# Five moves of work in a pooling and retention step: states, k and v, gates, pooling sums, stores

## The chip, the cores and the metric

The kernel runs on 1 core of one Trainium2 chip. The metric is the device time in microseconds, the median of several runs. Lower is better.

## What is computed

One step of a hybrid decoder layer, for a prompt of 2048 tokens and for 8 sample sequences of 4 new tokens each, all in float32:

```python
h = rmsnorm(x, g_norm)
u_p, z_p, q, k, v, z_r, gates = split(h @ w_in)        # widths 1024,1024,1024,1024,2048,2048,2048
pooled = windowed means of u_p (windows 2, 4, 8, 16; one per group of 256) - u_p
pooled = einsum(pooled, w_pool_group) * pool_scale
y_pool = (pooled * silu(z_p)) @ w_branch_pool
o, s_new = retention(rope(q), rope(k) * 256**-0.5, v, s_old)   # 4 heads, Dk 256, Dv 512
y_ret = (groupnorm(o) * gn_ret * silu(z_r)) @ w_branch_ret
merged = sigmoid(gate_p) * y_pool + sigmoid(gate_r) * y_ret
y = rmsnorm(x + merged @ w_out, g_final)               # also returned: the last 15 rows of u, s_new
```

The prompt begins with empty states. The samples begin with `state_pool` (8 x 15 x 1024) and `state_ret` (8 x 4 x 256 x 512, 16 MB), and the new states are stored.

## The kernel before

**How it works.** Every product is made of float32r matmuls on split operands: high part, and low part = value - high. One product of 128 x 128 weights by 512 tokens takes three matmuls. ScalarE makes the high parts, VectorE the low ones. All engines run programs written out by hand in a fixed order, and semaphores that count finished steps tie them together. There are three stages.

**Stage A** (to about 1656 us of the span) projects the prompt through `w_in`. It runs over two halves of 1024 tokens and, in each, 40 jobs of 256 columns: per head q, v, k, v, zp, u, z, z, and eight gate jobs. A job is seven block products (a Strassen-like scheme; slots 0 to 6 are A11B11, A12B21, S2T2, S1T1, S3T3, S4B22, A22T4) of twelve matmuls each. VectorE's program at each slot i is: evict the product of this slot (slots 1, 4, 5), make the low part of the weights six products ahead, then a piece of the post-processing of the job before. ScalarE does likewise (evictions at 0, 2, 3, 6; highs of weights; sigmoids). The last product (slot 6) writes the bank that slot 4's eviction empties (`c22_done`); slot 2 (S2T2) waits for ScalarE's copy of slot 0's product (`part_s`, `s_copied`). For a "u" job, VectorE computes windowed sums in `windows(j, t, first, end)`: steps k = 0 to g (head g) are sums over shifted copies, k = g + 1 is the final that writes `c_out`; step 0 also copies 16 columns. The second part of tokens (t = 1) is handled during the next job, a z job. That z job's `z_sigmoid(j, 0)`, at the end of slot 6 on ScalarE, writes `tmp`, which shares its place with `win_a` and `win_b`, so it waits for the final. Results go to DRAM (`qk_d`, `kt_d`, `v_d`, `z_d`, `pool_d`, `zp_d`, `gate_d`).

**Stage B** (to about 2752 us) runs over four blocks of 512 tokens. Per head: `update(hb, 0)`, `output(hb, 0)`, `turn_og(hb - 1)` (transposes), `update(hb, 1)`, `branch(hb - 1, 0)`, `output(hb, 1)`, `scores(hb + 1)`, `branch(hb - 1, 1)`; hb counts heads over all blocks. Behind the last head come group mixing, the branch and the output projections. `gate_og(hb)` on VectorE multiplies four banks of transposed outputs by the gate z (line 2261) and makes their low parts; the high parts are ScalarE's. `branch(hb, 0)` overwrites those four banks, so it waits for all four gatings, and before quarter vt for its low part. SyncE issues the loads in program order; a wait holds all that is behind it. At the passage from A to B it loads head 1's q and k^T scores operands, four weight units, stores the last gate, waits for everything, and only then loads head 1's k and v for the updates (`head_piece(0, 1, 2..5)`).

**The samples' stage** (from about 2752 us) runs over four heads. Per head: panels of weights come through a ring of eight buffers `s_w` (SyncE); TensorE multiplies them by the tokens; the states `s_in` (8 samples, 512 KB each) are read by the output matmuls (line 1573), updated by VectorE with TensorE's `update`, multiplied by a decay on ScalarE (`scaled(h, q)`, into one of four buffers `s_out`), and stored by GpSimd, which waits for each scaling. Before sample 0 to 3 of the next head ScalarE waits (`s_stored`) until GpSimd has seen all stores land; before sample 4 to 7 until the store of four samples before has. Behind `scaled(h, 4)` ScalarE makes the highs of the z panel. The tail projects and normalises the samples.

Of the kernel before, what the change touches and what calls it, by code (L numbers as in the profile page):

```python
# [208 lines left out]
def build(nc, io):  # L209
    with ExitStack() as ctx:  # L210
# [302 lines left out]
        s_stored = Steps(sem("s_stored"), [], in_heads(["states"]), [])  # L513
# [162 lines left out]
        def _(sp):  # L676
# [226 lines left out]
            for what in ("q", "k"):  # L903
                stored(sp, max(j for j in range(ALL) if JOBS[j] == (what, 1, 0)))
            for n in range(2):
                head_piece(0, 1, n)
            for n in range(RAW):
                unit(0, n)
            store(ALL - 1)
# [11 lines left out]
            head_gates(0, 0)  # L921
# [3 lines left out]
            for n in range(2, 6):  # L925
                head_piece(0, 1, n)
# [3 lines left out]
            for n in range(RAW, LEAD):  # L930
                unit(0, n)
# [103 lines left out]
            results(NB - 1)  # L1035
# [3 lines left out]
            load_states(0, seqs)  # L1039
            for h in range(HEADS):  # L1040
                if h:
                    load_qkv(h)
                    load_states(h, (7,))
                if h == HEADS - 1:
                    for k in range(4):
                        load_pair(pair("mix", None, k), io["w_pool_group"][0, k], GW)
                load_columns("z", h, h * DV + COL_ZR)
                for p in range(2):
                    name, first = (("u", COL_U), ("zp", COL_ZP), ("gp", COL_G), ("gr", COL_G + D))[h]
                    load_columns(f"{name}{p}", None, first + 512 * p)  # L1050
                    load_states(h + 1, ((0, 1, 2), (3, 4))[p])
                for p in range(2):
                    for k in range(2):
                        load_pair(pair("br", h, 2 * p + k),
                                  io["w_branch_ret"][0][h * DV + k * 2 * P:h * DV + (k + 1) * 2 * P, p * 512:(p + 1) * 512])
                load_states(h + 1, (5, 6))
                if h == 0:
                    sp.wait_ge(out_stored, 16 * NT * NB)
                    sp.dma_start(s_gate_b[:].rearrange("p g c -> p (g c)"), io["b_gate"].broadcast_to([S, 2 * D]))\
                        .then_inc(s_gate_in, 16)  # L1060
                    sp.dma_start(s_pool_s[:], io["pool_scale"].broadcast_to([S, D])).then_inc(s_gate_in, 16)
# [6 lines left out]
        def _(pool):  # L1068
# [92 lines left out]
            for s in (s_pow, s_stored):  # L1161
                pool.sem_inc(s.sem, s.credit)
# [17 lines left out]
            for h in range(HEADS):  # L1180
# [3 lines left out]
                for q in seqs:  # L1184
                    if q == 5:
                        inverse_std("head", h, "var_eps")
                    pool.wait_ge(s_act.sem, s_act.done("head", h, f"scaled{q}"))
                    pool.dma_start(io["ret_sample"][0, q, h].rearrange("(k p) v -> p k v", p=P), s_out[:, q % 4])\
                        .then_inc(s_state_out[q % 4], 16)

                if h + 1 < HEADS:
                    pool.dma_start(s_c[:], io["c_sample"][h + 1]).then_inc(s_c_in, 16)
                    pool.dma_start(s_decay[:], io["c_sample_decay"][h + 1]).then_inc(s_c_in, 16)
                for k in range(4):
                    pool.wait_ge(s_state_out[k], (h + 1) * (16 * SB // 4))
                pool.sem_inc(s_stored.sem, 1)
# [9 lines left out]
            pool.wait_ge(s_c_in, 32 * HEADS)  # L1206
            pool.wait_ge(out_stored, 16 * NT * NB)
# [406 lines left out]
        def _(act):  # L1614
# [321 lines left out]
            def scaled(h, q):  # L1936
                wait("head", h, f"new{q}_1")
                if q < 4:
                    act.wait_ge(s_stored.sem, s_stored.done("head", h, None))
                else:  # L1940
                    act.wait_ge(s_state_out[q % 4], h * (16 * SB // 4) + 16)
                do(s_out[:, q % 4], s_in[:, q], scale=s_decay[:, 0:1])

# [43 lines left out]
        def _(dve):  # L1987
# [173 lines left out]
            for j in range(ALL):  # L2161
                for i in range(PROD):
# [4 lines left out]
                    if j and kind(j - 1) == "u":  # L2167
                        if i < 3:
                            windows(j - 1, 0, 2 + i, 3 + i)
                        elif i == 3:  # L2170
                            windows(j - 1, 1, 0, 2)
                        else:
                            windows(j - 1, 1, i - 2, i - 1)
# [81 lines left out]
            def gate_og(hb):  # L2255
                s, h = hb % 2, hb % HEADS
                dve.wait_ge(z_arrived[s], 32 * (hb // 2 + 1))
                for vt in range(5):
                    if vt < 4:
                        dve.wait_ge(ogt_mm, 4 * hb + vt + 1)  # L2260
                        dve.scalar_tensor_tensor(out=z_in[s][:, vt, :], in0=banks[2 + vt][:],  # L2261
                                                 scalar=ret_g[:, h, vt:vt + 1], in1=z_in[s][:, vt, :],
                                                 op0=ALU.mult, op1=ALU.mult).then_inc(og_gated, 1)
                    if vt:
                        dve.wait_ge(og_hi_done, 4 * hb + vt)
                        tt(z_lo[s][:, vt - 1, :], z_in[s][:, vt - 1, :], og_hi[:, vt - 1, :].bitcast(F32),
                           ALU.subtract, og_lo_done)
# [334 lines left out]
            for p, bank in enumerate((4, 5)):  # L2602
# [5 lines left out]
                if p == 0:  # L2608
                    lows_of("out0", None, range(3))
# [40 lines left out]
```

## Time and profile before

| | |
|---|---|
| median of 3 runs | 3061.72 us (3061.45, 3061.72, 3066.86) |
| the profiled execution | 3067.94 us, span 3066.2 us |
| TensorE matmul busy | 2969.4 us, 97% |
| VectorE busy | 1875.3 us, 61% |
| ScalarE busy | 1183.9 us, 39% |
| GpSimd busy | 710.7 us, 23% |
| HBM | read 410.63 MB, written 169.50 MB, 189 GB/s over the span |
| chain that ended last | TensorE 83%, VectorE 7%, DMA 5%, issue 3% |

A row of the timeline gives the start, the length, the engine, the line of the kernel, the operation with its output and inputs, and in brackets the idle time of the engine before it and who ended it. SPq and POOL DMA rows are issues, not transfers. Matmuls are pipelined: rows overlap, and the time that one takes from the engine is the distance of two starts.

### The profile page before, as it was taken

How to read it: one execution, taken by the hardware profiler on the slowest of the kernel's cores; microseconds unless marked ns; L12 is line 12 of the kernel's file. 1: busy time of each engine (PE TensorE's matmuls, PEld its weight loads, DVE VectorE, ACT ScalarE, POOL GpSimd, SP SyncE). 2: the span in 40 equal slices, each digit the busy share in tenths (PEclk: the TensorE clock that was granted, in tenths of full speed). 3: DMA queues.
4: the chain of work that ended last, by engine and by line, in shares of the span. 5: the costliest groups of instructions: out<-in, count | busy, mean ns of one | idle time of the engine just before them, and what ended most of it. 6: DMA issues, size and time to landing. Idle time of an engine off the chain costs nothing.

```text
span 3066.2 us, 35792 instructions
## 1 busy us (share of the span) xinstructions
PE 2969.4 (97%) x13064; PEld 2303.6 (75%) x13064; DVE 1875.3 (61%) x2625; ACT 1183.9 (39%) x1925; POOL 710.7 (23%) x501
## 2 busy tenths in 40 slices
PE   6999999999999999999999999999999999998997
PEld 5888888888778888888887888888888888872332
DVE  8666576765464756566665674657567566653435
ACT  5434444445554444443443333323333333332223
POOL 5242524344332344343432000000000000001110
PEclk9999999999999999999999999999999999999999
DMA  4535354436543453444446546635554564649885
GB/s 133 206 121 189 131 186 145 165 128 201 186 165 124 151 179 138 163 156 156 160 163 238 221 160 246 275 133 186 228 221 151 219 253 163 212 158 367 304 307 210
DMA packets 297542, 582.14 MB, mean 190 GB/s; under 512 B 24777, under 2 KB 167625, under 8 KB 286192
## 3 DMA queue, kind: packets, MB, share of 16 engines
q1 hardware_dynamic: 292039, 562.73, 51.8%
q0 software_dynamic: 5328, 17.12, 1.4%
q8 instruction: 106, 1.74, 0.2%
q14 instruction: 69, 0.56, 0.1%
HBM read 410.63 MB, written 169.50 MB: 189 GB/s over the span
## 4 chain that ended last, share of the span: by engine, by line
PE 83%; DVE 7%; DMA 5%; issue 3%; ACT 1%; POOL 1%; SPq 0%; DVEq 0%; ACTq 0%; POOLq 0%
PE bank L1224 25%; PE bank L1226 24%; PE bank L1225 24%; PE bank L1512 4%; DMA raw<-in_w_branch_pool 2%; PE bank L1573 2%; PE bank L1272 1%; DMA s_w<-in_w_in 1%; DVE z_in L2261 1%; DVE win_a L1989 1%; DVE wa_lo L1989 1%; DVE z_lo L1989 1%; DVE c_out L1989 1%; PE bank L1566 1%; DVE xs L2003 1%
## 5 line engine op out<-in xcount | busy, mean ns | idle before, releaser
L1224 PE MATMUL bank<-xa_hi,wa_hi 128*128 128x512 f32 x2240 | 885.4, 395 | 12.5 <-DVE c_out L1989 8.1
L1226 PE MATMUL bank<-xa_hi,wa_lo 128*128 128x512 f32 x2240 | 875.4, 391 | 0.0
L1225 PE MATMUL bank<-xa_lo,wa_hi 128*128 128x512 f32 x2240 | 874.7, 390 | 0.0
L1224 PEld LDWEIGHTS bank<-xa_hi,wa_hi 128*128 128x128 f32 x2240 | 421.8, 188 | 100.5 <-issue 15.8
L1226 PEld LDWEIGHTS bank<-xa_hi,wa_lo 128*128 128x128 f32 x2240 | 421.4, 188 | 88.8
L1225 PEld LDWEIGHTS bank<-xa_lo,wa_hi 128*128 128x128 f32 x2240 | 421.9, 188 | 83.7
L1989 DVE TENSOR_TENSOR wa_lo<-w_raw,wa_hi 128x512 fp32r<-128x512 f32 x320 | 313.0, 980 | 192.9 <-ACT wa_hi L1667 191.4
L1989 DVE TENSOR_TENSOR wa_lo<-w_sum,wa_hi 128x512 fp32r<-128x512 f32 x240 | 195.2, 813 | 224.6 <-ACT wa_hi L1667 224.6
L1989 DVE TENSOR_TENSOR w_lo<-raw,w_hi 128x512 fp32r<-128x512 f32 (+1 forms) x288 | 180.4, 660 | 221.4 <-ACT w_hi L1775 221.2
L1667 ACT ACTIVATE wa_hi<-w_raw 128x512 fp32r<-128x512 f32 x320 | 200.9, 628 | 245.7 <-PE bank L1226 242.1
L1775 ACT ACTIVATE w_hi<-raw 128x512 fp32r<-128x512 f32 (+1 forms) x288 | 165.7, 603 | 270.8 <-PE bank L1226 102.7
L1156 POOL TENSOR_TENSOR inv_std<-var_eps,half 128x2 f32<-128x2 f32 x32 | 25.7, 802 | 943.2 <-DVE var_eps L2246 943.2
L1108 POOL TENSOR_TENSOR w_sum<-w_raw,w_sum 128x512 f32<-128x512 f32 x80 | 127.1, 1588 | 382.3 <-DVE wa_lo L1989 380.4
L1224 PE MATMUL bank<-og_hi,w_hi 128*128 128x512 f32 x512 | 205.0, 400 | 9.2 <-DVE z_in L2261 9.2
L1225 PE MATMUL bank<-z_lo,w_hi 128*128 128x512 f32 x512 | 203.0, 396 | 0.0
L1226 PE MATMUL bank<-og_hi,w_lo 128*128 128x512 f32 x512 | 201.8, 394 | 0.0
L1667 ACT ACTIVATE wa_hi<-w_sum 128x512 fp32r<-128x512 f32 x240 | 150.4, 627 | 122.3 <-PE bank L1226 115.2
L1114 POOL TENSOR_TENSOR w_sum<-w_raw,w_sum 128x512 f32<-128x512 f32 x80 | 105.7, 1322 | 289.6 <-DVE wa_lo L1989 289.6
L1120 POOL TENSOR_TENSOR c_out<-c_out,tmp 128x1024 f32<-128x1024 f32 x48 | 118.7, 2475 | 196.1 <-ACT tmp L1711 196.1
L1989 DVE TENSOR_TENSOR c_out<-bank,part_s 128x512 f32<-128x512 f32 x144 | 99.0, 687 | 96.5 <-PE bank L1226 64.9
L1103 POOL TENSOR_TENSOR w_sum<-w_raw 128x512 f32<-128x512 f32 x80 | 124.2, 1553 | 73.1 <-DVE wa_lo L1989 64.9
L1110 POOL TENSOR_TENSOR w_raw<-w_raw 128x512 f32<-128x512 f32 x80 | 134.0, 1674 | 0.0
(261 smaller groups left out, 4711.7 us busy)
## 6 DMA issues: line engine op xcount, KB each, us to landing
w_raw<-in_w_in SPq DMA_DIRECT2D x80, 1024.0 KB, 5.1
v_d<-turned SPq DMA_DIRECT2D x64, 512.0 KB, 3.2
qk_s<-qk_d SPq DMA_DIRECT2D x32, 1024.0 KB, 7.5
v_s<-v_d SPq DMA_DIRECT2D x32, 1024.0 KB, 10.9
raw<-in_w_branch_ret SPq DMA_DIRECT2D x128, 256.0 KB, 3.9
s_w<-in_w_in SPq DMA_DIRECT2D x64, 512.0 KB, 8.6
tabs<-in_c_rope SPq DMA_DIRECT2D x16, 1024.0 KB, 6.6
qk_d<-high SPq DMA_DIRECT2D x32, 512.0 KB, 4.6
```

Of the source, the lines that this page charges most:

```text
L1103: pool.tensor_tensor(w_sum[:, 0], b12, b11, ALU.subtract).then_inc(w_summed, 1)
L1108: pool.tensor_tensor(w_sum[:, 1], b22, w_sum[:, 0], ALU.subtract).then_inc(w_summed, 1)
L1110: pool.tensor_tensor(b12, b22, b12, ALU.subtract).then_inc(w_summed, 1)
L1114: pool.tensor_tensor(w_sum[:, 1], b21, w_sum[:, 1], ALU.subtract).then_inc(w_summed, 1)
L1120: pool.tensor_tensor(c_out[:, j % 2, t], c_out[:, j % 2, t], tmp[t][:], ALU.mult).then_inc(z_mul, 1)
L1224: pe.matmul(out, lh, rh, start=first, stop=False, skip_group_check=onto)
L1225: pe.matmul(out, lh, rl, start=False, stop=False, skip_group_check=onto)
L1226: return pe.matmul(out, ll, rh, start=False, stop=last, skip_group_check=onto)
L1512: mm = pe.matmul(banks[bank][0:lhs.shape[-1], at_col:at_col + width], lhs, s_w[:, m % SRING, k % 2, 0:width], start=first, stop=last)
L1667: act.activation(wa_hi[:, n % SLOTS], src, ACT.Copy).then_inc(wa_hi_done, 1)
L1775: act.activation(w_hi[:, u % RING, 0:width], raw[:, u % RAW, 0:width], ACT.Copy).then_inc(w_hi_done, 1)
L1989: return dve.tensor_tensor(out, a, b_, op).then_inc(s, 1)
```

## The change

Five edits, on the same computation.

- **Stage A, pooling sums** (t = 1): at slot 3 only step 0 (before: 0 and 1), at slots 4 and 5 steps 1 and 2 (before: 2 and 3), at slot 6 steps 3 and 4 (before: 4).
- **A to B, SyncE's order**: head 1's q, k, and k, v of its first chunk, then head 0's gate, the last store, four weight units, k and v of the second chunk; the waits for everything come behind these. The wait for the stores of head 1's q and k jobs goes.
- **Stage B, `gate_og`**: four gatings, then four low parts, in place of gate, gate, low, gate, low, gate, low, low.
- **Samples, SyncE**: `load_states(0, ...)` comes before the stores of the last block's results. **Samples, ScalarE**: each scaling is followed by a wait for its own end and the issue of its store, on ScalarE's queue; GpSimd no longer issues these 32 stores, and the semaphore `s_stored` is gone: ScalarE waits only for the store that used the same buffer.
- **Tail, VectorE**: the third low part of the out0 weights comes behind the second half of `s_g` in place of behind the first.

```diff
-            for what in ("q", "k"):
-                stored(sp, max(j for j in range(ALL) if JOBS[j] == (what, 1, 0)))
-            for n in range(2):
+            for n in range(4):
                 head_piece(0, 1, n)
+            head_gates(0, 0)
+            store(ALL - 1)
             for n in range(RAW):
                 unit(0, n)
-            store(ALL - 1)
+            for n in range(4, 6):
+                head_piece(0, 1, n)
...
             sp.wait_ge(win_step, win_steps(NS, 0, 0))
-            head_gates(0, 0)
             stored(sp, ALL - 2)
             stored(sp, ALL - 1)
             all_turned_stored(sp, ALL)
-            for n in range(2, 6):
-                head_piece(0, 1, n)
+            for n in range(RAW, LEAD):
+                unit(0, n)
...
-            results(NB - 1)
             sp.wait_ge(m_added, KT * NB)
             sp.wait_ge(pg_lo_done, KT * NB)
             sp.wait_ge(mix_mm, KT * NB)
             load_states(0, seqs)
+            results(NB - 1)
...
-                for q in seqs:
-                    if q == 5:
-                        inverse_std("head", h, "var_eps")
-                    pool.wait_ge(s_act.sem, s_act.done("head", h, f"scaled{q}"))
-                    pool.dma_start(io["ret_sample"][0, q, h].rearrange("(k p) v -> p k v", p=P), s_out[:, q % 4])\
-                        .then_inc(s_state_out[q % 4], 16)
-
+                inverse_std("head", h, "var_eps")
+
+                pool.wait_ge(s_act.sem, s_act.done("head", h, f"scaled{SB - 1}"))
...
-                for k in range(4):
-                    pool.wait_ge(s_state_out[k], (h + 1) * (16 * SB // 4))
-                pool.sem_inc(s_stored.sem, 1)
...
                 wait("head", h, f"new{q}_1")
-                if q < 4:
-                    act.wait_ge(s_stored.sem, s_stored.done("head", h, None))
-                else:
-                    act.wait_ge(s_state_out[q % 4], h * (16 * SB // 4) + 16)
+                if h or q >= 4:
+                    act.wait_ge(s_state_out[q % 4], 16 * (2 * h + q // 4))
                 do(s_out[:, q % 4], s_in[:, q], scale=s_decay[:, 0:1])
+                wait("head", h, f"scaled{q}", s_act)
+                act.dma_start(io["ret_sample"][0, q, h].rearrange("(k p) v -> p k v", p=P), s_out[:, q % 4])\
+                    .then_inc(s_state_out[q % 4], 16)
...
                         if i < 3:
                             windows(j - 1, 0, 2 + i, 3 + i)
-                        elif i == 3:
-                            windows(j - 1, 1, 0, 2)
                         else:
-                            windows(j - 1, 1, i - 2, i - 1)
+                            windows(j - 1, 1, i - 3, i - 2 if i < PROD - 1 else GROUPS + 1)
...
-                for vt in range(5):
-                    if vt < 4:
-                        dve.wait_ge(ogt_mm, 4 * hb + vt + 1)
-                        dve.scalar_tensor_tensor(... z_in[s][:, vt, :] ...).then_inc(og_gated, 1)
-                    if vt:
-                        dve.wait_ge(og_hi_done, 4 * hb + vt)
-                        tt(z_lo[s][:, vt - 1, :], ..., ALU.subtract, og_lo_done)
+                for vt in range(4):
+                    dve.wait_ge(ogt_mm, 4 * hb + vt + 1)
+                    dve.scalar_tensor_tensor(... z_in[s][:, vt, :] ...).then_inc(og_gated, 1)
+                for vt in range(4):
+                    dve.wait_ge(og_hi_done, 4 * hb + vt + 1)
+                    tt(z_lo[s][:, vt, :], ..., ALU.subtract, og_lo_done)
...
                 if p == 0:
-                    lows_of("out0", None, range(3))
+                    lows_of("out0", None, range(2))
+            lows_of("out0", None, (2,))
             wait("tail", 0, "m_t", s_act)
```

## Rows read from the trace of the kernel before

**Rows 1.** View by line, TensorE: busy us, mean ns, idle before and releasers.
```profile
L1224 PE MATMUL bank<-xa_hi,wa_hi 128*128 128x512 f32 x2240 | 885.4, 395 | 12.5 <-DVE c_out L1989 8.1 <-ACT part_s L1674 3.4 <-DVE wa_lo L1989 0.8
...
L1224 PE MATMUL bank<-og_hi,w_hi 128*128 128x512 f32 x512 | 205.0, 400 | 9.2 <-DVE z_in L2261 9.2
```

**Rows 2.** Timeline 1611 to 1623 (start us, length us), behind a pooling job.
```profile
1612.23 1.25 DVE L1989 TENSOR_TENSOR win_b<-win_a 128x1050 f32<-128x1050 f32 x1
...
1612.66 0.39 PE L1225 MATMUL bank<-xa_lo,wa_hi 128*128 128x512 f32 x1
...
1612.88 0.39 PE L1226 MATMUL bank<-xa_hi,wa_lo 128*128 128x512 f32 x1
...
1613.40 0.68 DVE L1989 TENSOR_TENSOR c_out<-bank,part_s 128x512 f32<-128x512 f32 x1
...
1614.22 0.47 PE L1224 MATMUL bank<-xa_hi,wa_hi 128*128 128x512 f32 x1 [0.95 <-DVE c_out L1989]
...
1618.41 0.69 DVE L1989 TENSOR_TENSOR wa_lo<-w_raw,wa_hi 128x512 fp32r<-128x512 f32 x1 [0.24 <-ACT wa_hi L1667]
...
1619.11 1.22 DVE L2121 SCALAR_TENSOR_TENSOR c_out<-win_b,ext 128x1024 f32<-128x1024 f32 x1
...
1621.68 0.58 ACT L1674 ACTIVATE part_s<-bank 128x512 f32<-128x512 f32 x1
```

**Rows 3.** Timeline, gating of two prompt heads, at 1958 and 2083.
```profile
1958.18 1.41 DVE L2261 SCALAR_TENSOR_TENSOR z_in<-bank,ret_g,z_in 128x512 f32<-128x512 f32 x2
...
1959.63 0.69 DVE L1989 TENSOR_TENSOR z_lo<-z_in,og_hi 128x512 fp32r<-128x512 f32 x1
...
1961.23 0.39 PE L1226 MATMUL bank<-v_s,kt_s 128*128 128x512 f32 x1
...
1962.30 0.50 PE L1224 MATMUL bank<-og_hi,w_hi 128*128 128x512 f32 x1 [0.68 <-DVE z_in L2261]
...
2083.67 0.49 PE L1224 MATMUL bank<-og_hi,w_hi 128*128 128x512 f32 x1 [0.19 <-DVE z_in L2261]
```

**Rows 4.** Timeline 1673 to 1694, heads 0 and 1 of block 0.
```profile
1673.33 1.43 SPq L862 DMA_DIRECT2D v_s<-v_d  x1
...
1675.74 0.69 DVE L1989 TENSOR_TENSOR sc<-bank,mask 128x512 f32<-128x512 f32 x1 [0.74 <-PE bank L1226]
...
1680.65 0.79 PE L1224 MATMUL bank<-v_s,kt_s 128*128 128x512 f32 x1 [4.94 <-DMA v_s<-v_d]
...
1684.86 0.69 DVE L2221 COPY state<-bank 128x512 f32<-128x512 f32 x1
...
1689.63 1.41 DVE L2261 SCALAR_TENSOR_TENSOR z_in<-bank,ret_g,z_in 128x512 f32<-128x512 f32 x2
...
1693.75 0.50 PE L1224 MATMUL bank<-og_hi,w_hi 128*128 128x512 f32 x1 [0.69 <-DVE z_in L2261]
```

**Rows 5.** Stretches (last: PEclk, DMA share, GB/s), then timeline lines.
```profile
2754.00:2756.00 2.00, 2.00 (x6) 0.85 (x5) 2.00 (x2) 0.00 (x0) 2.00 (x4) 1.00 0.05 14
...
2759.18 5.91 SPq L1029 DMA_DIRECT2D s_in<-in_state_ret  x8
...
2824.16 6.23 PE L1512 MATMUL bank<-s_w,sx 128*128 128x512 f32 x7 [5.77 <-DMA s_w<-in_w_in]
```

**Rows 6.** Timeline 2774 to 2787, samples' head 0; then DMA landings (us).
```profile
2774.33 1.15 ACT L1843 ACTIVATE s_out<-s_in,s_decay 128x1024 f32<-128x1024 f32 x1 [6.16 <-DVE s_in L2343]
...
2785.38 3.89 ACT L1930 ACTIVATE s_hi<-s_w 128x1024 fp32r<-128x1024 f32 x4
...
2786.71 4.62 DVE L1989 TENSOR_TENSOR s_lo<-s_w,s_hi 128x1024 fp32r<-128x1024 f32 x4
...
out_ret_sample<-s_out POOLq DMA_DIRECT2D x8, 512.0 KB, 6.8
...
DMA to landing us min/median/max: 3.9/10.6/17.2
```

**Rows 7.** Timeline 3040, the samples' tail.
```profile
3040.33 0.68 PE L1448 MATMUL bank<-ident,s_g 32*128 32x32 f32 x8 [3.31 <-DVE s_g L2343]
```

More of the change, by code:

```diff
@@ L512, in build @@
         s_pow = Steps(sem("s_pow"), ["x"], in_heads(["o"]), ["out"])
-        s_stored = Steps(sem("s_stored"), [], in_heads(["states"]), [])
         s_mm = Steps(sem("s_mm"), ["x_t", "hist"],
@@ L929, in _ @@
                 .then_inc(b_consts_in, 16)
-            for n in range(RAW, LEAD):
-                unit(0, n)
             def ahead(b, first, end):
@@ L1158, in _ @@
                             inverse_out(b - 1)
-            for s in (s_pow, s_stored):
-                pool.sem_inc(s.sem, s.credit)
+            pool.sem_inc(s_pow.sem, s_pow.credit)
             def inverse_std(part, h, name):
@@ L1206, in _ @@
             pool.wait_ge(s_c_in, 32 * HEADS)
+            for k in range(4):
+                pool.wait_ge(s_state_out[k], HEADS * (16 * SB // 4))
             pool.wait_ge(out_stored, 16 * NT * NB)
@@ L2257, in gate_og @@
                 dve.wait_ge(z_arrived[s], 32 * (hb // 2 + 1))
-                for vt in range(5):
-                    if vt < 4:
-                        dve.wait_ge(ogt_mm, 4 * hb + vt + 1)
-                        dve.scalar_tensor_tensor(out=z_in[s][:, vt, :], in0=banks[2 + vt][:],
-                                                 scalar=ret_g[:, h, vt:vt + 1], in1=z_in[s][:, vt, :],
-                                                 op0=ALU.mult, op1=ALU.mult).then_inc(og_gated, 1)
-                    if vt:
-                        dve.wait_ge(og_hi_done, 4 * hb + vt)
-                        tt(z_lo[s][:, vt - 1, :], z_in[s][:, vt - 1, :], og_hi[:, vt - 1, :].bitcast(F32),
-                           ALU.subtract, og_lo_done)
+                for vt in range(4):
+                    dve.wait_ge(ogt_mm, 4 * hb + vt + 1)
+                    dve.scalar_tensor_tensor(out=z_in[s][:, vt, :], in0=banks[2 + vt][:],
+                                             scalar=ret_g[:, h, vt:vt + 1], in1=z_in[s][:, vt, :],
+                                             op0=ALU.mult, op1=ALU.mult).then_inc(og_gated, 1)
+                for vt in range(4):
+                    dve.wait_ge(og_hi_done, 4 * hb + vt + 1)
+                    tt(z_lo[s][:, vt, :], z_in[s][:, vt, :], og_hi[:, vt, :].bitcast(F32), ALU.subtract, og_lo_done)
             def add_y(hb, p):
```

## The prediction

> **What bounds the kernel now.** I read the share of busy time first, then TensorE's groups by line with the idle time before them, then the list of TensorE's gaps in its timeline, and around each kind of gap the timeline of all engines; for the samples' stage also the DMA share by stretch. TensorE is busy 97% of the span, so only its gaps can be won or lost. The two largest kinds that a releaser explains by VectorE stand in [rows 1]: 8.1 us behind the evictions of line 1989 in stage A and 9.2 us behind the gating of line 2261. The rest that matters here are single waits for DMA (4.94 us in [rows 4], 5.77 us in [rows 5]) and one of 3.31 us in the tail [rows 7]. In the prompt stages matmuls start 0.22 to 0.23 us apart [rows 2], so a gap costs its start-to-start time less 0.23.
>
> **Pooling sums.** There are 8 "u" jobs (4 heads, 2 halves), and in the job behind each TensorE stops once. [rows 2] show the last: the sum k=1 (1612.23, 1.25 us) sits ahead of the eviction of product S3T3 (1613.40, 0.68), whose bank the last product wants at 1612.88 + 0.23 = 1613.11; it starts at 1614.22. Loss 1.11 us. The change moves k=1 behind that eviction, which can then start at 1612.2 and end at 1612.8: no wait. What is late next is the end of the sums. For heads 0 and 1 they end before the last product and cost nothing. For head 2 the final moves into the last product (slot 6): a low of weights waits for ScalarE, which follows TensorE; it starts 4.19 us after the last product's start (1618.41 against 1614.22), the final starts 0.70 later (1619.11), lasts 1.22, and ScalarE's copy to part_s starts 1.35 after its end (1621.68) and lasts 0.58. That is 8.04 us after the last product's start, plus about 0.15 for the semaphore; the product that needs it starts after 3 x 12 x 0.2275 = 8.19. Just hidden. For head 3 one more sum (1.2 us) is in slot 6: 9.2 to 9.4, so TensorE waits about 1.0 there. It waits at the next job's third product for ScalarE, which stands in front of z_sigmoid for tmp. So 6 jobs win 1.11 and 2 win 0.1 to 0.2: **7.0 us** (ends: 4.8 if head 2 is late too, 8.9 if none is).
>
> **Gates in one piece.** [rows 3]: gating starts at 1958.18 and today runs gate, gate, low, gate, low, gate, with 0.66 us between starts of gates and 0.61 behind a low; TensorE starts 4.12 us later (1962.30), once all four banks are read. Now it is four gates (2.64) and one low (0.61 to 0.69, +0.05): 3.35 to 3.4, so 1961.55. It could have started at 1961.23 + 0.23 = 1961.46. Win 0.75. The later lows come every 0.61 us, TensorE takes 2.7 us for each, and VectorE's whole chain of eight operations keeps its length, so who is queued behind (bias, state_low) sees no change. There are 12 such gaps of 1.07 to 1.11 us (three heads, four blocks): 9.0. The four last heads have a smaller one (2083.67, idle 0.19; start to start 0.58): the whole gap of 0.35 goes, 1.4. Sum **10.4 us** (8 to 11).
>
> **Head 1's k and v.** SyncE issues v at 1673.33, behind a wait for the last gate's store; TensorE is ready at 1675.55 and starts at 1680.65 [rows 4]. After the change k and v are issued at about 1656.6, behind 3.5 MB of other loads; at the 400 GB/s of a full stretch they are in by 1671. That wait of 5 us goes, but what is late next is VectorE: it masks head 1's scores until 1675.74 + 0.69, which TensorE waits for too (start 1676.5), then has the statistics of head 0 and four lows of branch weights, and copies the new state at 1684.86 without having waited for TensorE. The two copies, two bn_stats and their small operations need 0.6 + 0.6 + 0.6 + 1.03 = 2.85 us, so gating starts at 1687.7 instead of 1689.63. Win **1.9 us**, not 5; with the one-piece gates branch(0, 0) starts at 1691.1, not 1693.75. z_in and the four weight units, moved among these loads, land by about 1678, and are wanted from 1681.8 on: nothing. Ends 1 and 5.
>
> **Samples' states sooner.** The DMA engines are idle at 2754 to 2756 (share 0.05), between the load of q, k, v and the results' stores; the states follow at 2759.18 [rows 5]. From 2758 to 2824 they are full, and TensorE's waits for s_w (1.1 us in the u panels, 1.5 at the branch, 5.9 before head 1's q and k at 2824.16) come at the end of that backlog. Issued at 2747.4, the states fill the hole: shares of 0.88, 0.05, 0.74 over three stretches of 2 us leave 2.7 us of DMA time, and all that stands behind comes 2.7 us sooner. The stores of results move behind the states and nobody waits for them. What is left of the last wait (5.9 less what does not reach it) still takes the clock down (granted 0.50, that is 1.2 GHz, in 2824 to 2828). Win **2.7 us** (0 to 7: with the clock kept, 4 more).
>
> **Stores from ScalarE.** The trace has no DMA issued by ScalarE. SyncE's issue of the same shape takes 5.91/8 = 0.74 in a burst [rows 5], 0.37 at least. Per sample ScalarE then needs 1.15 + 0.1 + 0.37 to 0.74, below the 2.5 us in which TensorE delivers samples. But behind scaled(4) stand the highs of z: hi at 2785.38, low at 2786.71, TensorE at 2788.27, almost without slack [rows 6]. One wait for its own end and one issue put 0.5 to 0.8 us ahead of them; 0.3 of it was slack of VectorE in heads 0 to 2, none in head 3. Cost 3 x 0.25 + 0.55 = **1.3 us** (0 to 5, the upper end with issues of 1.3 us). The three scalings of samples 5 to 7 grow by 2 us, with 7 us before their reader. GpSimd's queue only loses work; s_c and s_decay keep their place in time.
>
> The row says that landing depends on the queue: 6.8 us median on GpSimd's, 10.6 for states on SyncE's. The Trainium skill, "DMA: Bandwidth & Descriptors", section "Issuing engines are not separate DMA queues", says that DMAs of all engines share the same 16 DMA engines and that issuing from another engine saves only issue time. By it this part wins nothing in bandwidth, which is also what the sum has; by a reading in which the stores went faster the sum would be lower by what DMA waits are left, up to 5 us.
>
> **Tail.** One low of 4.62/4 = 1.15 us [rows 6] leaves the place ahead of s_g of half 1, for which TensorE waits 3.31 us [rows 7]; it now runs while TensorE transposes and ScalarE copies s_mt (0.7 + 0.4 us). Win **1.1 us** (0.9 to 2.6; the matmuls behind it run 0.63 instead of 0.39 long, at half the clock, and a shorter wait may spare that).
>
> **Sum.** 7.0 + 10.4 + 1.9 + 2.7 - 1.3 + 1.1 = 21.8 us. All gains of the prompt stages lie in local chains that start at TensorE, so each passes on to the end. The profiled execution took 3067.94 us (span 3066.2) and would take 3046; it is 6.2 above the median of the runs, 3061.72, which the forecast goes by: **3040 us**.
>
> **Rivals.** (1) ScalarE's issues are dear, or head 2's pooling is late too: 3.7 + 2.2 us less won, 3046, with runs to 3050. For it: no row of such an issue, slack of 0.0 to 0.1. (2) More than the sum: the clock is kept at 2824 and in the tail, 4 + 1.5 us more, 3034. Against it: of the wait at 2824 more than 3 us stay. (3) Slower: ScalarE's stores land as late as SyncE's loads when queued, up to 17.2 us [rows 6]. scaled(4) needs the buffer of sample 0; its store is issued about 2775.6 and today's start is 2784.33, so it hides landings up to 8.7 us. At 17.2 each head loses 8.5, four heads 34: 3074. It decides from (L - 8.7) x 4 = 22, L = 14.2. Against it: ScalarE never has more than two or three stores queued, and heads 1 to 3 begin with DMA engines half idle. (4) The moves don't do what they say: pooling stops only change their place for all heads, and the DMA hole is filled by nothing useful: 7 + 2.7 less, 3050 to 3056.
>
> **Chances.** Forecast 0.60 (3035 to 3045), (1) 0.18, (2) 0.10, (3) 0.03, (4) 0.09. Range 3031 to 3053: it takes in (1), most of (2) and half of (4), and the 5 us by which the runs shown differ only in part. 0.2% is 6.1 us, about what a measurement of this kernel can tell from no change; faster by more than that (under 3055.6) 0.92, within 0.05, slower 0.03.
>
> **What would show it.** In the changed trace: the gap at the last product behind u jobs gone, and a gap of about 1 us before the third product of the next job for head 3 only, released by part_s; gaps at branch(hb, 0) of 0.3 us, released by a low; update(1, 0) starting at the mask's end and branch(0, 0) 2.6 us earlier; the DMA share without a hole, the wait before head 1's q and k still 5 to 6 us; z highs 0.6 us later in each sample head; the tail's wait near 2.2 us. The prediction is wrong if ScalarE's s_out waits for DMA, or if gaps of 1 us come back at another product of stage A.

## The result and the profile after

The changed kernel takes 3040.76 us (median of four runs, 3038.15 to 3046.85), before 3061.72: a ratio of 0.9925, interval 0.9911 to 0.9939, so 0.6 to 0.9% faster. On a second chip the unchanged file gave 3041.37 against 3065.37 (0.9919, 0.9905 to 0.9933). The profiled execution took 3038.15 us, span 3036.4, against 3067.94 and 3066.2. As before's profiled run lay above its median and this one below, 29.8 us separate the two traces, and only 21 to 24 the medians. A second profile of the changed kernel (the run e12_after_again) has a span of 3040.2; where one stretch is read closely, both are given.

The view by line has lost the two kinds of gaps of [rows 1]. Columns: count, busy us, mean ns of one, idle us before them and releasers. The matmuls of line 1224 are at line 1215 now:

```profile
PE 2962.3 (98%) x13064; PEld 2300.4 (76%) x13064; DVE 1873.1 (62%) x2625; ACT 1185.8 (39%) x1925; POOL 688.6 (23%) x469
...
L1215 PE MATMUL bank<-xa_hi,wa_hi 128*128 128x512 f32 x2240 | 884.3, 395 | 6.3 <-ACT part_s L1665 5.2 <-DVE wa_lo L1981 1.0
...
L1215 PE MATMUL bank<-og_hi,w_hi 128*128 128x512 f32 x512 | 204.2, 399 | 1.0 <-DVE y L2262 0.7 <-issue 0.2
```

c_out and z_in have gone as releasers (8.1 and 9.2 us). part_s went from 3.4 to 5.2, which is the new wait behind the pooling jobs of head 3.

TensorE's marks, the same instruction found in each trace (us; the last column is the sum of the prediction split in the same way):

| stretch | before | after | after again | won | forecast |
|---|---|---|---|---|---|
| start to head 0's first v_s, kt_s matmul (stage A) | 1659.26 | 1651.61 | 1653.69 | 7.7, 5.6 | 7.0 |
| to branch(0, 0) | 34.49 | 31.85 | 31.82 | 2.6, 2.7 | 2.6 |
| to the samples' first panel | 1058.65 | 1049.76 | 1049.86 | 8.9, 8.8 | 9.7 |
| to head 1's q and k panel | 71.76 | 68.49 | 68.17 | 3.3, 3.6 | 2.7 |
| to the tail's s_g transposes | 216.17 | 212.87 | 213.26 | 3.3, 2.9 | -0.2 |
| to the last matmul | 14.00 | 12.51 | 14.09 | 1.5, -0.1 | 0 |
| to the issue of y_sample's store | 4.71 | 4.76 | 4.76 | 0 | 0 |
| to the end of the span | 7.12 | 4.51 | 4.50 | 2.6, 2.6 | 0 |

Two stretches won what the sum did not have: the one to the tail and the end of the span. The rows of after that answer to those of before, all of the timeline (start us, length us, in brackets idle before and releaser). First head 3's pooling, at the third product of the next job [rows 2], then the crossing to stage B [rows 4]:

```profile
667.87 0.47 PE L1215 MATMUL bank<-xa_hi,wa_hi 128*128 128x512 f32 x1 [0.71 <-ACT part_s L1665]
...
1614.87 0.47 PE L1215 MATMUL bank<-xa_hi,wa_hi 128*128 128x512 f32 x1 [1.00 <-ACT part_s L1665]
...
1693.69 1.28 ACT L1766 ACTIVATE w_hi<-raw 128x512 fp32r<-128x512 f32 x2 [6.46 <-DMA raw<-in_w_branch_ret]
1698.91 1.16 ACT L1766 ACTIVATE w_hi<-raw 128x512 fp32r<-128x512 f32 x2 [3.93 <-DMA raw<-in_w_branch_ret]
...
1703.32 0.50 PE L1215 MATMUL bank<-og_hi,w_hi 128*128 128x512 f32 x1 [0.69 <-DVE y L2262]
```

The rows show the wait of about 1 us that was forecast, and one that wasn't: the branch weights land late behind head 1's k and v, ScalarE's highs come in two late pairs, VectorE's y behind them, and TensorE stops at 1703.32 (0.97 us from start to start, so 0.74 is handed back; 0.76 idle in the second profile).

Then the samples' stage: head 1's q and k panel [rows 5] with the clock around it (last columns of a stretch: granted clock, DMA share, GB/s), head 3's z panels, and the tail [rows 7]:

```profile
2801.71 2.93 PE L1503 MATMUL bank<-s_w,sx 128*128 128x512 f32 x3 [5.10 <-DMA s_w<-in_w_in]
...
2798.00:2802.00 4.00, 0.29 (x1) 0.29 (x2) 0.00 (x0) 0.00 (x0) 0.40 (x1) 0.64 1.10 317
2802.00:2806.00 4.00, 4.00 (x5) 1.55 (x5) 0.00 (x0) 0.00 (x0) 0.00 (x0) 0.50 1.10 337
...
2734.00:2736.00 2.00, 2.00 (x6) 0.88 (x5) 1.35 (x2) 0.00 (x0) 2.00 (x4) 1.00 0.95 377
...
2973.65 0.39 PE L1521 MATMUL bank<-s_hi,sx_hi 128*32 128x512 f32 x1 [1.10 <-DVE s_lo L1981]
...
3014.58 0.62 PE L1439 MATMUL bank<-ident,s_g 32*128 32x32 f32 x7 [1.80 <-DVE s_g L2331]
```

The DMA hole is filled (0.95 in the stretch that answers to the 0.05 of before). The wait of 5.8 us is now 5.1 (4.8 in the second profile) and the granted clock still falls to 0.50 behind it. ScalarE's stores, of which before had no row (the group of all 32, issue ns min/median/max, then the landing us):

```profile
L1933 ACTq DMA_DIRECT2D out_ret_sample<-s_out x32: 378/379/467, 2756.3 to 2984.3; - x32
...
DMA to landing us min/median/max: 2.8/7.5/10.9
...
  ACT s_out L1834: 4.1, 8
  ACT s_hi L1921: 2.0, 4
```

An issue costs 0.38 to 0.47 us. The last two lines say who waited for a scaling: ScalarE itself, 0.5 us before each of the eight scalings that nothing else delayed, and 0.5 before each of the four s_hi. In this kernel no scaling waits for a DMA.

### The profile page after: what moved, and what is told of

It is laid out like the page before. It is cut to its first block, busy times and chain, and to the rows that moved or that the text cites. A ratio compares the mean times of both kernels' runs of the same rounds, so it can differ in the third digit from the quotient of the medians.

```text
span 3036.4 us, 35782 instructions
## 1 busy us (share of the span) xinstructions
PE 2962.3 (98%) x13064; PEld 2300.4 (76%) x13064; DVE 1873.1 (62%) x2625; ACT 1185.8 (39%) x1925; POOL 688.6 (23%) x469
## 4 chain that ended last, share of the span: by engine, by line
PE 87%; DMA 4%; DVE 4%; issue 2%; ACT 1%; POOL 1%; SPq 1%; ACTq 0%; DVEq 0%; POOLq 0%
PE bank L1215 26%; PE bank L1217 26%; PE bank L1216 25%; PE bank L1503 4%; DMA raw<-in_w_branch_pool 2%; PE bank L1564 2%; PE bank L1263 1%; DMA s_w<-in_w_in 1%; PE bank L1371 1%; DVE wa_lo L1981 1%; PE bank L1557 1%; DMA raw<-in_w_branch_ret 1%; DVE xs L1995 1%; DVE xa_lo L1981 0%; PE bank L1521 0%
```

## The experiments

The theory is that of the prediction: the parts are local, and their gains add up. The rivals are that parts take their gain from one another, or that the gain beyond the sum belongs to one of them. e1 to e4 ran on one chip, where before took 3063.91 us, e5 to e8 on another with 3066.01, e9 to e12 on a third with 3065.37, so times of different chips are compared by their ratio to before. A gain in us is one minus that ratio, times before's median.

**Pooling alone** (before with this edit):

```diff
-                        elif i == 3:
-                            windows(j - 1, 1, 0, 2)
                         else:
-                            windows(j - 1, 1, i - 2, i - 1)
+                            windows(j - 1, 1, i - 3, i - 2 if i < PROD - 1 else GROUPS + 1)
```

> The kernel before with the shift of the pooling sums alone. My theory (local waits, head 3's sums end too late): the six waits of about 1 us behind the u jobs of heads 0 to 2 go, the two of head 3 are replaced by waits for part_s of 0.7 and 1.0 us; stage A ends 7.0 to 7.7 us sooner, all of it reaches the end, 3054 to 3055 us. Rival (the stops only change their place): the waits come back for head 2 as well or for all heads, 0 to 5 us, 3057 to 3062.

Measured: 0.9975 (0.9965 to 0.9986), 7.7 us less (4.3 to 10.7). The line of stage A:

```profile
L1224 PE MATMUL bank<-xa_hi,wa_hi 128*128 128x512 f32 x2240 | 883.5, 394 | 6.6 <-ACT part_s L1674 5.9 <-DVE wa_lo L1989 0.6
```

8.1 us of c_out are gone, part_s is up by 2.5, and stage A ends at 1650.46 against 1659.26. The six profiles without this edit end stage A anywhere from 1659.3 to 1662.3 (mean 1660.4), and the six with it and no other edit of stage A from 1650.5 to 1655.1 (mean 1652.4). So one profile can't give the size to a microsecond; the means lie 8.0 us apart, one above the forecast of 7.0.

**Gates alone** (before with `gate_og` as four gatings and then four lows, as in the diff of the change):

> The kernel before with the gates in one piece alone. My theory: twelve waits of 0.7 us before branch(hb, 0) go but for some 0.1, and four of 0.2: 10 us, 3051 to 3052. In the first block head 1 hangs on VectorE's chain, which the order inside the gating does not shorten, yet its first low comes 0.75 earlier all the same. Rival (weights' loads or the later lows take the gain back, as the wait of 0.69 us before the second half of the branch in the changed kernel hints): up to 2 us less in each block, 3054 to 3058.

Measured: 0.9964 (0.9951 to 0.9977), 11.0 us less (7.0 to 15.0). z_in is gone as a releaser of branch matmuls:

```profile
L1224 PE MATMUL bank<-og_hi,w_hi 128*128 128x512 f32 x512 | 204.1, 399 | 0.1
```

Branch(0, 0) comes 0.76 us sooner after the start of stage B and the rest of the prompt takes 1049.32 in place of 1058.65: 10.1 us, for the 10.4 of the sum. The gaps of 0.3 us released by a low, which the prediction named as a sign, didn't come: 0.1 us is all the idle time of this line.

**Head 1's k and v alone** (before with the two parts of the diff that change SyncE's order at the crossing):

> The kernel before with SyncE's new order at the passage from stage A to B alone. My theory: the wait of 4.94 us for v goes, but VectorE's queue (mask, statistics, four lows, copies) sets the next start, so branch(0, 0) comes 1.9 us sooner and no more, 3059.8. Rival (the transfer was the bound): 5 us sooner at branch(0, 0), 3056.7. A third: what is gained is lost behind head 2's loads, which now meet the branch's weights sooner: 1 us or less.

Measured: 0.9994 (0.9985 to 1.0004), 1.8 us less with an interval on both sides of nothing; this and the next are below what the runs can settle, and the trace has to speak. TensorE's rows at the crossing:

```profile
1686.63 0.47 PE L1222 MATMUL bank<-v_s,kt_s 128*128 128x512 f32 x1 [2.37 <-DVE state L2219]
...
1692.14 0.50 PE L1222 MATMUL bank<-og_hi,w_hi 128*128 128x512 f32 x1 [0.93 <-DVE z_in L2259]
```

The DMA wait of 4.94 us is gone, a wait of 2.37 for VectorE's state stands in its place, and branch(0, 0) comes 1.98 us sooner after the start of stage B (32.51 against 34.49). In the kernels that keep the old order and the old gating this stretch runs from 33.0 to 34.6, as the wait for v_s varies (3.50 to 5.19).

That VectorE sets the new start, and not TensorE, can be read from the seven profiles with both this order and the new gating. In five of them the granted clock fell to 0.50 for some 2 us behind the wait of 2.37 us, in two (e10_store3_gpsimd and e11_store3_scalar) it stayed at 1.00 up to there, TensorE was ready sooner and waited for the gating:

```profile
1686.89 0.47 PE L1231 MATMUL bank<-og_hi,w_hi 128*128 128x512 f32 x1 [1.84 <-DVE z_in L2267]
```

Yet branch(0, 0) came 31.82 to 31.86 us after the start of stage B in all seven.

The wait for y at the branch's second half is 0.19 us here and is in no row of the run with the gates alone; only both together make it the 0.69 of the changed kernel. There two parts do take something from each other, about half a microsecond.

**States alone** (before with `load_states(0, ...)` ahead of the results):

```diff
-            results(NB - 1)
...
             load_states(0, seqs)
+            results(NB - 1)
```

> The kernel before with the samples' states ahead of the results' stores alone. My theory: 2.7 us of idle DMA time are filled, the waits for s_w before head 1's q and k end 2.7 to 3.3 us sooner, the last of them stays above 4 us and still takes the granted clock to 1.2 GHz for a while; 3058 to 3059. Rival (the hole is filled, but SyncE's queue or the DMA backlog gives it back): no change at head 1's q and k, 3061.7. Second rival (the clock is kept): 7 us, 3054.7.

Measured: 0.9996 (0.9987 to 1.0005), 1.2 us less. The hole is filled, and the panel waits less:

```profile
2754.00:2756.00 2.00, 2.00 (x6) 0.95 (x5) 1.92 (x2) 0.00 (x0) 2.00 (x4) 1.00 0.78 300
...
2820.61 1.22 PE L1512 MATMUL bank<-s_w,sx 128*128 128x512 f32 x1 [4.38 <-DMA s_w<-in_w_in]
```

From the first panel to head 1's q and k: 67.95 us. Over all profiles the kernels without this edit take 69.0 to 71.8 (mean of six 70.7), those with it in the changed kernel's order of loads 67.3 to 69.4 (mean of seven 68.4). So it is 2.3 us by the means, where the sum had 2.7, and single profiles of kernels alike in this stage differ by as much.

**Stores alone** (before with the stores on ScalarE's queue), and the reverse, **the changed kernel with the stores back on GpSimd**. In both GpSimd's program and `s_stored` change with it as in the change above; the lines on ScalarE are

```diff
                 do(s_out[:, q % 4], s_in[:, q], scale=s_decay[:, 0:1])
+                wait("head", h, f"scaled{q}", s_act)
+                act.dma_start(io["ret_sample"][0, q, h]..., s_out[:, q % 4]).then_inc(s_state_out[q % 4], 16)
```

> The kernel before with the 32 stores of new states issued by ScalarE alone. My theory: an issue costs ScalarE 0.4 to 0.5 us behind each scaling and 0.1 for its own end; heads 0 to 2 start z 0 to 0.3 us later, head 3 0.5 to 0.6; 1 us slower or the same, 3062 to 3063. Rival (the queue matters for the transfers: stores land sooner and weights too): the DMA waits before head 1 shrink, 3057 to 3060. Open from the two profiles: the end behind the last transfer took 4.4 us before and 1.8 after; if GpSimd's long list of DMAs is the cause, this kernel alone shows 1.8 there, 2.6 us sooner, 3059 to 3060 in sum.

> The changed kernel with the stores of new states back on GpSimd. If ScalarE's issues cost 1 us in all, this is 1 us faster than the changed kernel in the heads (head 3's z starts 0.6 us sooner), 3039.8. If the 2.6 us at the very end hang on GpSimd's DMAs, it is 2.6 slower there, 3042.4 in sum. If the stores from GpSimd slow the loads, head 1's q and k come later than 68.5 us behind the first panel.

Measured: alone 0.9988 (0.9978 to 0.9997), 3.7 us faster (0.9 to 6.7) where the prediction had 1.3 slower. The reverse has a ratio of 0.9916 (0.9898 to 0.9933), no different from the changed kernel's 0.9925 and 0.9919. So the medians don't settle the size, nor the sign in the second pair; the traces agree on where a gain sits. From the issue of y_sample's store to the end of the span it is 4.51 us with ScalarE's stores and 7.12 with GpSimd's, in both pairs (after and the reverse; the run alone and before). (The 4.54 and 7.15 of the expectations take the span as printed, rounded to 0.1 us.) That last store itself is issued by GpSimd in all four and lands 2.2 us after its issue in all four. Against it stands the cost: in head 3 the z panels wait 1.10 us for s_lo with ScalarE's stores, 0.48 with GpSimd's, again in both pairs; in heads 0 to 2 no such wait shows. Over the whole way from the first panel to the tail's s_g the kernels with ScalarE's stores are slower by more than that 0.6: 281.4 us in both profiles of the changed kernel against 280.1 in the reverse, 288.7 in the run alone against 287.9 before. The waits for panels vary by as much from profile to profile, so the cost lies between 0.6 and 1.3 us and the net gain between 1.3 and 2.0.

**Tail alone** (before with the third low part of the out0 weights behind the second half of s_g):

> The kernel before with the third low of out0 behind the second half of s_g alone. My theory: the wait before the transposes of s_g falls from 3.31 to about 2.2 us, 1.15 us sooner; whether the out panels then run at full clock decides over 1.5 more. 3059 to 3060.6. Rival (the low is wanted as soon as the product starts, and delays it there): no gain, 3061.7.

Measured: 0.9995 (0.9986 to 1.0005), 1.5 us less. The s_g wait:

```profile
3036.95 0.68 PE L1448 MATMUL bank<-ident,s_g 32*128 32x32 f32 x8 [1.80 <-DVE s_g L2343]
...
3040.00:3044.00 4.00, 4.00 (x12) 1.67 (x11) 1.54 (x3) 2.12 (x2) 0.00 (x0) 0.58 0.00 0
```

3.31 us became 1.80 (2.27 in the second profile of the changed kernel). Before's profile is at the long end: in four of the other five with the old order this wait is 2.94 us and in the fifth 3.01, and against these the edit gives 1.1, as forecast. The clock still falls to 0.58 behind it. From s_g to the last matmul this kernel needs 14.09 us, before 14.00.

**The sigmoids later** (the changed kernel; ScalarE copies part_s before the first half of the sigmoid of the job behind a pooling job). It asks whether the new 1 us waits of head 3 are ScalarE's order only:

```diff
                     if i == 0 and j and kind(j - 1) in ("z", "zp"):
+                        if j > 1 and kind(j - 2) == "u":
+                            z_sigmoid(j - 1, 0)
                         z_sigmoid(j - 1, 1)
...
-                    if kind(j) in ("z", "zp") and i == A22T4:
+                    if kind(j) in ("z", "zp") and i == A22T4 and not (j and kind(j - 1) == "u"):
```

> The changed kernel with ScalarE's z_sigmoid of the first half behind the copy of part_s of the next job, for the z job behind a u job only. If head 3's two waits for part_s (0.71 and 1.00 us) come from the final that holds z_sigmoid, which stands in front of part_s, they go: 1.7 us sooner at the end of stage A, 3039. If they come from the number of VectorE's operations or from shared reads with GpSimd, they stay or move to c_out or wa_lo, 3040.8. Risk: GpSimd's silu starts later and the weights' sums behind it too; then new waits for w_sum, up to 1 us each of 16.

Measured: 0.9910 (0.9894 to 0.9925), 3038.84 us. The interval overlaps that of the changed kernel (0.9905 to 0.9933), so the medians don't show a gain; the trace shows that the two waits went. TensorE has no gap of 0.5 us or more between 1611 and 1648, nor between 600 and 700, and stage A ends at 1648.20 (1649.10 in the next run, which has this edit too), where the changed kernel's two profiles have 1651.61 and 1653.69. So the two waits came from ScalarE's order. The wait of 2.25 us for part_s at 862.79, at the start of the second half of the tokens, is another: here it stands under a different name, and in the next run it is there again as 2.25 us for part_s.

```profile
860.55 0.77 PE L1215 MATMUL bank<-xa_hi,wa_hi 128*128 128x512 f32 x1 [2.69 <-DVE xa_lo L1983]
```

**Head 1's panel first** (with the sigmoids later as well; the states of samples 5 and 6, the gate bias and the pooling scale go behind the next head's q, k, v on SyncE's queue), beside **the changed kernel again**:

```diff
-                    load_states(h, (7,))
+                    load_states(h, (5, 6, 7))
+                if h == 1:
+                    sp.wait_ge(out_stored, 16 * NT * NB)
+                    sp.dma_start(s_gate_b[:].rearrange("p g c -> p (g c)"), ...).then_inc(s_gate_in, 16)
+                    sp.dma_start(s_pool_s[:], io["pool_scale"].broadcast_to([S, D])).then_inc(s_gate_in, 16)
...
-                load_states(h + 1, (5, 6))
-                if h == 0:
-                    sp.wait_ge(out_stored, 16 * NT * NB)
-                    sp.dma_start(s_gate_b[:].rearrange("p g c -> p (g c)"), ...).then_inc(s_gate_in, 16)
-                    sp.dma_start(s_pool_s[:], io["pool_scale"].broadcast_to([S, D])).then_inc(s_gate_in, 16)
```

> The kernel after with two moves: z_sigmoid(j, 0) stands behind the next job's part_s copy on ScalarE where a u job comes before (as in the run with the sigmoids late), and on SyncE's queue the states of the next head's samples 5 and 6, the gate bias and the pooling scale go behind that head's q, k and v panels. If head 1's q and k panel is late only because of what SyncE issues before it, TensorE's wait for it falls from 5.10 us (after) or 5.49 us (sigmoids late) to about 1.6 us, the clock in the 4 us behind it stays at 1.00 instead of 0.50, and the time falls by 3 to 6 us against the kernel after: 3033 to 3037 us. The rival: the sixteen queues carry a share above 1.0 there for some 50 us, so bandwidth decides and the bytes that go later are missed by states of head 1; then the wait stays above 4 us or comes back at new0_1's scaling of head 1, and the time is 3037 to 3040 us.

> The kernel after, unchanged, on the same chip as the runs beside it, for their comparison: 3038 to 3043 us, y_sample's DMA issued 4.5 us before the end of the span.

Measured: 3033.09 us (3031.1 to 3034.08), 0.9894 (0.9880 to 0.9908) of before, against 3041.37 (3038.66 to 3041.94) for the changed kernel on the same chip. That is 8 us less with both edits; against the run with the sigmoids alone it is about 5 (a ratio of 0.9894 against 0.9910). SyncE's rows in the changed kernel and then here, TensorE's panel, and its clock:

```profile
2782.39 2.84 SPq L1026 DMA_DIRECT2D s_in<-in_state_ret  x2
2785.27 2.05 SPq L1056 DMA_DIRECT2D s_gate_b<-in_b_gate  x1
2787.37 0.42 SPq L1058 DMA_DIRECT2D s_pool_s<-in_pool_scale  x1
2787.84 11.30 SPq L1016 DMA_DIRECT2D s_w<-in_w_in  x8
```

```profile
2780.86 9.81 SPq L1016 DMA_DIRECT2D s_w<-in_w_in  x8
...
2793.70 1.13 PE L1502 MATMUL bank<-s_w,sx 128*128 128x512 f32 x2
...
2792.00:2796.00 4.00, 4.00 (x11) 1.33 (x10) 0.68 (x1) 0.00 (x0) 0.78 (x1) 1.00 1.09 372
2796.00:2800.00 4.00, 4.00 (x11) 1.85 (x10) 0.00 (x0) 0.00 (x0) 0.00 (x0) 1.00 1.06 358
```

The panel has no wait at all, with the DMA share as high as in the changed kernel (1.09), and the clock stays at 1.00, that is 2.4 GHz. From the first panel to head 1's q and k it was 68.5 and 68.2 us and is 63.3; the 32 matmuls of that panel took 16.0 us and take 13.9.

So the rival falls, by which the transfers of the whole stretch set the time and the wait comes back elsewhere: no wait for a DMA is left in the heads behind it. Bytes still matter. The panel was late because of what SyncE had put ahead of it. Its first buffer lands 59.8 us after the first panel's start, where it took 66.3; SyncE issues it 4.1 us sooner, and it lands 9.3 us behind its issue in place of 11.7. Whether the 1 MB of states and the two small loads cost the panel this by their bytes or by SyncE's time to issue them (5.3 us) no run separates. Some of the gain is lost later: of the 7.3 us won by the end of that panel 5.8 are left at the tail's s_g (275.6 us from the first panel, for 281.4).

**The end of the span.** The stretch from y_sample's issue to the end goes by who issues the stores in every profile: 7.11 to 7.14 us in the seven with all 32 on GpSimd, 4.50 to 4.52 in the five with none. Two runs split them: head 3's eight stores on GpSimd and the rest on ScalarE, and the reverse. Each is the changed kernel with

```diff
-                wait("head", h, f"scaled{q}", s_act)
-                act.dma_start(...)
+                if h not in by_pool:
+                    wait("head", h, f"scaled{q}", s_act)
+                    act.dma_start(...)
```

where by_pool is [3] in the one and [0, 1, 2] in the other, and GpSimd issues those of by_pool (with two semaphores of their own).

> The kernel after with the eight stores of the last head's new states issued by GpSimd and those of heads 0 to 2 by ScalarE (two semaphores for GpSimd's, so that a scaling waits for a pair of stores). It asks what the stretch from the issue of y_sample's DMA to the end of the span hangs on: 7.15 us with all 32 stores on GpSimd, 4.54 us with none. If it grows with the number that GpSimd issued: 5.2 us. If it hangs on GpSimd's transfers near the end: 7.1 us. If it hangs on whether GpSimd issued any of them at all beyond its few small ones: 7.1 us too, and the run with heads 0 to 2 on GpSimd tells these two apart.

> The reverse of the run before: the 24 stores of heads 0 to 2 by GpSimd, the eight of the last head by ScalarE. If the stretch from the issue of y_sample's DMA to the end of the span grows with the number that GpSimd issued: 6.5 us. If it hangs on GpSimd's transfers near the end: 4.5 us. If on whether GpSimd issued any at all: 7.1 us.

Measured: 3044.17 and 3045.11 us. The span and the last row of GpSimd, first with 8 stores on GpSimd, then with 24:

```profile
core 0 of [0], span 3042.3 us
...
3037.16 0.56 POOL L1207 DMA_DIRECT2D out_y_sample<-s_x  x1 [1.60 <-DVE s_x L2351]
```

```profile
core 0 of [0], span 3041.8 us
...
3035.39 0.56 POOL L1207 DMA_DIRECT2D out_y_sample<-s_x  x1 [1.60 <-DVE s_x L2351]
```

and the same of the changed kernel, with none:

```profile
core 0 of [0], span 3036.4 us
...
3031.85 0.56 POOL L1193 DMA_DIRECT2D out_y_sample<-s_x  x1 [1.60 <-DVE s_x L2334]
```

With 0, 8, 24 and 32 of these stores the stretch is 4.51, 5.18, 6.46 and 7.12 us by the unrounded spans of the traces: (7.12 - 4.51)/32 = 0.082 us for each, which puts 8 at 5.2 and 24 at 6.5. It grows with the number that GpSimd issued, not with how late they were. All of it lies behind the landing of y_sample's store (2.27, 2.94, 4.24 and 4.89 us from there to the end); what is done in that time no row shows, nor whether it goes by stores, packets or bytes, as all 32 are alike. Both kernels took 3 to 4 us longer than the changed kernel beside them, of which the end explains 0.7 and 1.9. They also make a scaling wait for a pair of stores: with 24 stores on GpSimd three scalings wait 1.7 to 2.3 us for a store, with 8 none does. The rest is unexplained.

## Why the prediction was right, and where it wasn't

The time, 3040 forecast and 3040.8 measured, is right, and five of the six terms stand, in sign, place and roughly in size. That the two agree within a microsecond is luck. With the terms as the profiles have them the sum is 8.0 + 10.1 - 0.7 (the new wait at 1703.32) + 2.0 + 2.3 + 1.3 to 2.0 (stores) + 1.2 = 24.2 to 24.9 us and not 21.8; the interval of the ratio is a gain of 19 to 27 us and holds both.

- **Pooling, 7.0**: right in mechanism and place, 8.0 by the means of the profiles. All eight c_out gaps went, and head 3's wait for part_s came at the third product with 0.71 and 1.00 us. Head 2, "just hidden" with 0.15 us to spare, stayed hidden.
- **Gates, 10.4**: right, 10.1 in the trace of the run with this part alone, 11.0 by its medians.
- **Head 1's k and v, 1.9 and not 5**: right; the wait for v_s gave way to VectorE's chain, and branch(0, 0) came 2.6 us sooner with the gates, as worked out. "z_in and the four weight units ... nothing" was wrong by 0.7 us: branch weights that now stand behind head 1's loads landed after they were wanted (1703.32), most of it only with the gates changed too.
- **States, 2.7**: 3.3 and 3.6 at the panel in the two profiles, 2.3 by means over all. What was to be left of the wait (5 to 6 us, with the clock's fall) came as forecast: 5.1 and 4.8. The prediction put it down to a DMA backlog and didn't ask what the backlog held. e9_qk_first moved 1 MB of states and two small loads behind the panel's load, at the same DMA share, and the wait was gone with the clock's fall behind it.
- **Stores, -1.3**: the term of the wrong sign. Its cost was 0.6 us at head 3's z panels, where 0.55 was put down, and no wait shows in heads 0 to 2, where 0.75 was; over the whole of the heads the traces allow up to the 1.3 of the sum. An issue took 0.38 to 0.47, at the low end of the 0.37 to 0.74 taken. What was missing is the 2.6 us at the very end. "GpSimd's queue only loses work" was written, and priced at nothing; the end of the span turned out to grow with the stores that GpSimd issues, by what no row shows. Net it is +1.3 to +2.0 in place of -1.3. Rival (3) never came near: the longest landing on ScalarE's queue was 10.9 us, its median 7.5 against 6.6 for GpSimd's in before, and head 1's panel came no sooner with ScalarE's stores (68.5 and 68.2 us behind the first panel, 67.3 in the reverse). So there was nothing won in bandwidth, as the Trainium skill has it ("DMA: Bandwidth & Descriptors", section "Issuing engines are not separate DMA queues").
- **Tail, 1.1**: 1.5 and 1.0 in the two profiles, 1.5 alone, each against before's long wait of 3.31; 1.1 against the 2.94 of most others. Whether the clock then spares the output panels differs between profiles of one file (s_g to the last matmul 12.51 and 14.09 us). It did so in two of the eight profiles with this edit and in none of the six without it, which is too few to say whether the edit has a part in it; in the profile of the result it was luck at least in part.
- Left open: some 1.5 us between head 1's panel and the tail. Of the 3.3 and 2.9 won there the tail's wait is 1.5 and 1.0; the rest is there with the stores back on GpSimd too (212.75 us in e7), so it isn't theirs. It may be no effect at all: with the gates alone, which touch nothing in this stage, the stretch took 214.56 us, 1.6 less than the 216.17 of before.

## What to carry to other kernels

When a wait goes, ask what the next engine in the chain was doing meanwhile: head 1's k and v were worth 1.9 us and not the 5 that the wait was long, because VectorE had its own chain to finish. When a load is late in a stretch where the DMA engines are full, that need not bound the kernel: read what the issuing queue put ahead of that load, and move what isn't wanted yet behind it (5 us here and 2 more from the clock, of which 5.8 reached the tail). And a part that takes transfers off GpSimd is to be priced at the kernel's end too.

## What was not expected of the hardware

- The end of the span costs 0.08 us for each store of 512 KB that GpSimd issued, whenever it did: 4.51 us with none of the 32, 7.12 with all.
- A DMA issue on ScalarE took 0.38 to 0.47 us, and 0.5 us passed before a scaling or s_hi that stood behind a scaling and its store.
- After a wait of 4 to 6 us for head 1's panel TensorE was granted 0.50 (1.2 GHz) for the 4 us that follow, in before, after and e4, and 0.67 after 4.07 us in e7; without a wait there it stayed at 1.00. A shorter wait went either way: after 2.37 us at the crossing the clock fell to 0.50 in five profiles of the seven with both edits and stayed at 1.00 until TensorE's next wait in two, and after 1.80 us at s_g it fell to 0.58 in the tail's run and stayed at 1.00 in after.
